# One float32 matmul per weight product in place of a high/low split of three, with a ring of twelve tiles

## The chip, the cores and the metric

The kernel runs on one core of a Trainium2 chip. The metric is the device time in microseconds of one execution; the profile is of one execution of the same program.

## What is computed

Two blocks of a network on a sequence of 256 positions with 1024 channels, everything in float32. The first block, cut from its reference:

```
h = rms_norm(x, attn_norm_w)
z, xbc, dt_raw, q, k, v, g_ssd, g_att = split_columns(h @ w_in)            # 1024 x 7440
y_ssd = ssd_mixer(z, xbc, dt_raw, ...) @ w_ssd_out                          # 1024 x 1024
y_att = moba_attention(rope(q), rope(k), v) @ w_attn_out                    # 1024 x 1024
x = x + (sigmoid(g_ssd) * y_ssd + sigmoid(g_att) * y_att) @ w_out           # 1024 x 1024
h = rms_norm(x, moe_norm_w)
for g in range(4):                                                          # 4 groups of 8 experts
    hid = silu(einsum("bld,edf->blef", h, w_gate[g])) * einsum("bld,edf->blef", h, w_up[g])
    out = out + einsum("blef,ble,efd->bld", hid, comb[:, :, g], w_down[g])  # 256 wide
gate = sigmoid(rms_norm(x, ple_norm_w) @ w_ple_gate)                        # 1024 x 1024
```

The second block has an in-projection of 1024 x 7168, a causal convolution of 31 taps, a token shift with interpolation of three of its outputs, a recurrent mixer of 16 heads, three products of 1024 x 1024, and a feed-forward 1024 x 4096 x 1024 with a squared relu. Every weight is read once, some 228 MB in all, and the moving rows of a product are always the 256 positions.

## The kernel before

**Tiles of weights.** Weights are read in the order of use as tiles of 128 partitions x 1024 float32 (512 KB; 496 KB in the first in-projection), numbered by n from Q_IN to Q_END (lines 40 to 55). A tile holds two of the eight 128-row slices of a matrix by 512 columns (`pair_view`), in the experts half gate and half up (`gu_loads`), or one slice by 1024 columns. SyncE issues the loads (`load`) into a ring of 4 tiles, `raw`, which in the experts has two more tiles (`MOE_RING`, in `proj`). A load waits until the tile that it overwrites has been split, and one expert tile is two transfers.

**The split.** ScalarE copies each tile into `whi` (type float32r; `split_high`, line 270), then GpSimd, or for every second tile of the experts VectorE, writes raw minus whi into `wlo` (`split_low`, line 275). The other operand of a product, `t0` or `t1`, is split alike: TensorE transposes the activations into PSUM (class `Turn`, line 353), ScalarE writes the high half (line 364) and VectorE the low one (lines 372, 374). A product is then three matmuls that add up in PSUM (`times`):

```
nc.tensor.matmul(dst, hi, wh, start=first, stop=False)             # L281
nc.tensor.matmul(dst, hi, wl, start=False, stop=False)             # L282
return nc.tensor.matmul(dst, lo, wh, start=False, stop=last)       # L283
```

`wide_quarter` does this for one tile: two slices by two halves of the positions, so four products of 512 columns. The down part of the experts (lines 1397 to 1399) and the second part of the feed-forward (lines 2739 to 2741) do it in place. All other matmuls, transposes among them, have plain float32 operands.

**Order of the work.** Each engine has one program, written out stage by stage, and semaphores between them. `quarter_done` counts the tiles that TensorE has used. In the first in-projection (15 column tiles of four weight tiles; `pe_in`) TensorE puts parts of the mixer between the column tiles: after the fourth the transposes of xbc, after the seventh the decay sums (line 651), which wait for VectorE's convolution of four taps (lines 737, 739), and the transposes back (line 664). Then come the output product of the mixer, attention (a chain of small operations, lines 1050 to 1078), two products of 8 tiles, the router (`act_router`, `pe_router`, `dve_router`), and the experts. In the experts a block does the gate and up of expert E + 1 (4 tiles) and the down part of expert E (2 tiles); after the sixth expert of a group the rows of the next group are gathered (line 1341), and after the first of the next one the sum is scattered back (line 1446). Experts and feed-forward are loops (`Fori`) on all engines.

In the second in-projection (14 column tiles, `pe_in2`) VectorE first mixes the shifted rows (line 1990), then runs the convolution's 31 taps over seven slices (lines 2002, 2005; 217 operations, 120 of them first). From the ninth column tile on, ScalarE copies each result (line 1905) and starts a transfer from `proj` to `work` that moves it down by one row (line 1910); VectorE waits for it, subtracts (line 1956), multiplies with a row that ScalarE had loaded (line 1957) and adds (line 1960), and does 20 or 15 more operations of the convolution before the next one. ScalarE loads the row of the next column tile but one only when line 1957 has used the buffer, and this stands in its program before the next copy and transfer. The heads (`step_loop`, lines 2207 to 2283) and the feed-forward (`pe_out2`) end the kernel. GpSimd, besides splitting, rotates part of q and k (`pool_rotations`) and does a part of the heads (`pool_heads`).

Of the kernel before, what the change touches and what calls it, by code (L numbers as in the profile page):

```python
# [9 lines left out]
F32R = mybir.dt.float32r  # L10
# [18 lines left out]
RING = 4  # L29
MOE_RING = 6  # L30
# [118 lines left out]
JOB = 6 * 8  # L149


def split_by_vector(n):

    return Q_MOE - MOE_RING <= n < Q_PLE and n % 2 == 1


def slot(n):

    return (n - Q_MOE) % MOE_RING if Q_MOE <= n < Q_PLE else n % RING

RAW_DONE, LOW_DONE = [], []
_shown = [0] * MOE_RING
for _n in range(Q_END):
    _shown[slot(_n)] += 32 if Q_MOE <= _n < Q_PLE else 16
    RAW_DONE.append(_shown[slot(_n)])
    LOW_DONE.append(sum(split_by_vector(m) == split_by_vector(_n) for m in range(_n + 1)))


def at_turn(counts, n, i, per):

    if not per:
        return counts[n]
    span = JOB if per < JOB and JOB % per == 0 and n + JOB < Q_PLE and n >= Q_MOE - MOE_RING else per
    return counts[n] + (counts[n + span] - counts[n]) * per // span * i
# [6 lines left out]
def build(nc, A, out):  # L184
    ctx = ExitStack()
    with ctx:
# [8 lines left out]
        whi = sb("whi", [P, RING, QF], F32R)  # L195
        wlo = sb("wlo", [P, RING, QF], F32R)
# [4 lines left out]
        t0h = sb("t0h", [P, KC, SEQ], F32R)  # L201
        t0l = sb("t0l", [P, KC, SEQ], F32R)
        t1h = sb("t1h", [P, 4, SEQ], F32R)
        t1l = sb("t1l", [P, 4, SEQ], F32R)
# [30 lines left out]
        raw_full = [sem(f"raw_full{s}") for s in range(MOE_RING)]  # L235
        hi_ready = sem("hi_ready")
        lo_by_pool = sem("lo_by_pool")
        lo_by_dve = sem("lo_by_dve")
# [8 lines left out]

        more_raw = proj[:, :, :].rearrange("p t n -> p (t n)")[:, 12232:12232 + (MOE_RING - RING) * QF]

        def raw_of(n):  # L250

            s = slot(n)
            return raw[:, s, :] if s < RING else more_raw[:, (s - RING) * QF:(s - RING + 1) * QF]

        def wait_low(eng, n, i=0, per=0):

            eng.wait_ge(lo_by_dve if split_by_vector(n) else lo_by_pool, at_turn(LOW_DONE, n, i, per))
# [8 lines left out]
        def split_high(act, n, i=0, per=0, width=QF):  # L266
            s = n % RING
            act.wait_ge(raw_full[slot(n)], at_turn(RAW_DONE, n, i, per))
            wait_from(act, quarter_done, n - RING + 1 + per * i)
            nc.scalar.activation(whi[:, s, 0:width], raw_of(n)[:, 0:width], ACT.Copy).then_inc(hi_ready, 1)  # L270

        def split_low(eng, n, i=0, per=0, width=QF):
            s = n % RING
            eng.wait_ge(hi_ready, n + 1 + per * i)
            ins = (nc.vector if split_by_vector(n) else nc.gpsimd).tensor_tensor(  # L275
                wlo[:, s, 0:width], raw_of(n)[:, 0:width], whi[:, s, 0:width].bitcast(F32), ALU.subtract)
            ins.then_inc(lo_by_dve if split_by_vector(n) else lo_by_pool, 1)

        def times(dst, hi, lo, wh, wl, first, last):

            nc.tensor.matmul(dst, hi, wh, start=first, stop=False)  # L281
            nc.tensor.matmul(dst, hi, wl, start=False, stop=False)  # L282
            return nc.tensor.matmul(dst, lo, wh, start=False, stop=last)  # L283

        def pair_view(buf, n, width):
            return buf[:, n % RING, 0:2 * width].rearrange("p (k n) -> p k n", k=2)

        def wide_quarter(pe, n, q, dst, hi, lo, width=TW, i=0, per=0, begun=False):


            wait_low(pe, n, i, per)
            wh, wl = pair_view(whi, n, width), pair_view(wlo, n, width)
            for t in range(NT):
                for kk in range(2):
                    k = 2 * q + kk
                    mm = times(dst[t][:, 0:width], hi[:, k, t * P:(t + 1) * P], lo[:, k, t * P:(t + 1) * P],
                               wh[:, kk, :], wl[:, kk, :], k == 0 and not begun, k == KC - 1)
            mm.then_inc(quarter_done, 1)

        def load_square(sp, n, w, quarters=range(8), order="(p k) n -> p k n"):  # L300

            v = w.rearrange(order, k=KC)
            for j in quarters:
                c, q, m = j // 4, j % 4, n + j
                load(sp, m, [(pair_view(raw, m, TW), v[:, 2 * q:2 * q + 2, c * TW:(c + 1) * TW])])

        def square_product(pe, n, hi, lo, waits, turn=None):
# [4 lines left out]
            for c in range(2):  # L312
                for q in range(4):
                    if turn is not None and c == 0:
                        pe.wait_ge(*turn.done(2 * q + 2))
# [2639 lines left out]
```

## Time and profile before

| | before |
|---|---|
| time, median of 3 runs | 1740.38 us (1737.1 to 1743.37) |
| span of the profiled execution | 1741.1 us; no other time is given for that execution |
| instructions | 21017 |
| busy: ScalarE | 724.3 us, 42% |
| busy: VectorE | 932.0 us, 54% |
| moved by DMA | 239.91 MB, 138 GB/s over the span |
| GpSimd's line 275 | 331 subtractions of 128x1024 or 128x992, 856 us |
| the chain that ended last, by engine | TensorE 47%, VectorE 16%, GpSimd 15%, issue 13%, DMA 6%, ScalarE 3% |

The busy share says how long an engine had work in progress, matmuls overlapping each other counted once. The distance between the starts of two matmuls of one kind is what one costs in a row; the mean duration is longer, because they are pipelined. The granted clock is that of TensorE, as a share of its full speed. The DMA share is the mean busy share of 16 engines.

### The profile page before, as it was taken

The page shows a single profiled execution, that of the slowest core. Times are in us where ns is not written, and L with a number is a line of the kernel's source. Part 1 is how long each engine was busy: PE and PEld are TensorE (multiplying, and loading weights), DVE is VectorE, ACT ScalarE, POOL GpSimd, SP SyncE. Part 2 cuts the span into 40 slices and gives each one's busy share as a digit, 9 for nine tenths or more (in the row PEclk, how much of TensorE's full clock was granted, in tenths as well). Part 3 has the DMA queues.
Part 4 walks back from the last instruction along what each step waited for, and adds up shares of the span by engine and source line. Part 5 has one row for each costly group of instructions (what it writes and reads, how often), then busy time and mean ns, then how long its engine had stood idle before and what let it go on. Part 6 is the DMA issues. An engine that isn't in the chain of part 4 may idle for free.

```text
span 1741.1 us, 21017 instructions
## 1 busy us (share of the span) xinstructions
PE 1448.3 (83%) x6952; PEld 1180.4 (68%) x6952; DVE 932.0 (54%) x1343; ACT 724.3 (42%) x1212; POOL 896.3 (51%) x423
## 2 busy tenths in 40 slices
PE   6989987958988888797599983364899999879997
PEld 5878876747656667565477762253799997768885
DVE  1553444356978788794506995338566665320102
ACT  4455554334645455464543312224222332433433
POOL 6867574414867667683576532240300001748784
PEclk9989986989999999999899986685999999989998
DMA  6545440344977777683364332231200001535652
GB/s 218 176 132 157 127 142 0 97 143 142 301 227 259 232 244 255 226 291 117 121 209 146 116 102 74 74 108 36 85 2 0 0 0 59 161 100 177 192 180 85
DMA packets 126193, 239.91 MB, mean 138 GB/s; under 512 B 15236, under 2 KB 31286, under 8 KB 125996
## 3 DMA queue, kind: packets, MB, share of 16 engines
q1 hardware_dynamic: 116672, 228.17, 40.8%
q10 hardware_dynamic: 9453, 10.84, 2.0%
q8 instruction: 41, 0.67, 0.2%
q14 instruction: 27, 0.22, 0.0%
HBM read 234.79 MB, written 1.05 MB: 135 GB/s over the span
## 4 chain that ended last, share of the span: by engine, by line
PE 47%; DVE 16%; POOL 15%; issue 13%; DMA 6%; ACT 3%; ACTq 0%; POOLq 0%; DVEq 0%
POOL wlo L275 15%; PE bank L281 8%; PE bank L282 8%; PE bank L283 8%; DMA work<-proj 6%; DVE work L2005 5%; PE bank L2223 3%; PE bank L2241 2%; PE bank L2237 2%; PE bank L2207 2%; PE bank L2739 2%; PE bank L2741 2%; PE bank L2740 2%; DVE work L739 2%; DVE proj L1990 2%
## 5 line engine op out<-in xcount | busy, mean ns | idle before, releaser
L275 POOL TENSOR_TENSOR wlo<-raw,whi 128x1024 fp32r<-128x1024 f32 (+1 forms) x299 | 750.2, 2523 | 576.5 <-ACT whi L270 576.0
L281 PE MATMUL bank<-whi,t0h 128*128 128x512 f32 (+1 forms) x1072 | 447.1, 417 | 94.8 <-POOL wlo L275 71.2
L270 ACT ACTIVATE whi<-raw 128x1024 fp32r<-128x1024 f32 (+1 forms) x366 | 376.6, 1053 | 312.1 <-PE bank L283 230.2
L282 PE MATMUL bank<-wlo,t0h 128*128 128x512 f32 (+1 forms) x1072 | 432.6, 404 | 0.0
L283 PE MATMUL bank<-whi,t0l 128*128 128x512 f32 (+1 forms) x1072 | 431.9, 403 | 0.0
L281 PEld LDWEIGHTS bank<-whi,t0h 128*128 128x128 f32 x1072 | 209.3, 195 | 164.0 <-issue 80.1
L283 PEld LDWEIGHTS bank<-whi,t0l 128*128 128x128 f32 x1072 | 208.6, 195 | 49.5
L282 PEld LDWEIGHTS bank<-wlo,t0h 128*128 128x128 f32 x1072 | 208.7, 195 | 45.3 <-issue 1.7
L275 DVE TENSOR_TENSOR wlo<-raw,whi 128x1024 fp32r<-128x1024 f32 x67 | 185.3, 2767 | 39.4 <-ACT whi L270 39.2
L275 POOL TENSOR_TENSOR wlo<-proj,whi 128x1024 fp32r<-128x1024 f32 x32 | 105.8, 3308 | 30.9 <-ACT whi L270 30.9
L2005 DVE SCALAR_TENSOR_TENSOR work<-work,proj 128x256 f32<-128x256 f32 x210 | 113.1, 597 | 2.0
L2482 POOL TENSOR_TENSOR proj<-proj,small x8 | 5.1, 638 | 205.2 <-PE bank L2283 205.2
L275 DVE TENSOR_TENSOR wlo<-proj,whi 128x1024 fp32r<-128x1024 f32 x32 | 94.5, 2953 | 2.4 <-ACT whi L270 2.1
L1397 PE MATMUL bank<-whi,t1h 128*128 128x512 f32 x128 | 54.1, 423 | 32.7 <-POOL wlo L275 32.7
L2564 DVE TENSOR_TENSOR work<-bank,const 128x256 f32<-128x256 f32 x112 | 46.7, 423 | 63.8 <-PE bank L2223 60.8
L353 PE MATMUL bank<-const,work 128*128 128x128 f32 x128 | 27.3, 400 | 55.7 <-DVE work L433 45.5
L270 ACT ACTIVATE whi<-proj 128x1024 fp32r<-128x1024 f32 x64 | 67.4, 1055 | 10.0 <-PE bank L283 7.2
L2854 DVE TENSOR_TENSOR t1l<-bank,t1h 128x512 fp32r<-128x512 f32 x16 | 10.3, 686 | 112.9 <-ACT t1h L2811 112.9
L353 PEld LDWEIGHTS bank<-const,work 128*128 128x128 f32 x128 | 24.9, 220 | 58.1 <-DVE work L433 33.6
L1397 PEld LDWEIGHTS bank<-whi,t1h 128*128 128x128 f32 x128 | 24.4, 190 | 50.4 <-issue 26.4
L2241 PE MATMUL bank<-work 128*128 128x64 f32 x384 | 57.6, 276 | 0.7 <-DVE work L2564 0.7
L2408 ACT COPY work<-bank 128x128 f32<-128x128 f32 x80 | 21.4, 268 | 83.3 <-PE bank L2241 83.3
(416 smaller groups left out, 2142.5 us busy)
## 6 DMA issues: line engine op xcount, KB each, us to landing
raw<-in_w_ff SPq DMA_DIRECT2D x64, 512.0 KB, 3.5
raw<-in_w_exp_down SPq DMA_DIRECT2D x124, 256.0 KB, 3.9
raw<-in_w_in SPq DMA_DIRECT2D x60, 496.0 KB, 3.5
raw<-in_w_in SPq DMA_DIRECT2D x56, 512.0 KB, 3.4
raw<-in_w_exp_gate SPq DMA_DIRECT2D x66, 256.0 KB, 4.1
raw<-in_w_exp_up SPq DMA_DIRECT2D x66, 256.0 KB, 5.1
proj<-in_w_exp_gate SPq DMA_DIRECT2D x62, 256.0 KB, 3.5
proj<-in_w_exp_up SPq DMA_DIRECT2D x62, 256.0 KB, 5.1
```

Source lines behind the costliest of these rows:

```text
L270: nc.scalar.activation(whi[:, s, 0:width], raw_of(n)[:, 0:width], ACT.Copy).then_inc(hi_ready, 1)
L275: ins = (nc.vector if split_by_vector(n) else nc.gpsimd).tensor_tensor(wlo[:, s, 0:width], raw_of(n)[:, 0:width], whi[:, s, 0:width].bitca ...
L281: nc.tensor.matmul(dst, hi, wh, start=first, stop=False)
L282: nc.tensor.matmul(dst, hi, wl, start=False, stop=False)
L283: return nc.tensor.matmul(dst, lo, wh, start=False, stop=last)
L353: tr = nc.tensor.transpose(bank[4 + b][:, at:at + P], self.src[:, t, :, 2 * b + kk], ident)
L739: ins = nc.vector.scalar_tensor_tensor(out=convT[:, c, :], in0=xbcT[:, c, w:w + SEQ], scalar=tap, in1=convT[:, c, :], op0=ALU.mult, op1=AL ...
L1397: nc.tensor.matmul(bank[4 + h][:, :], hh, whi[:, s, f], start=first, stop=False, skip_group_check=True)
L2005: ins = nc.vector.scalar_tensor_tensor(out=cvT[:, c, :], in0=uT[:, c, w:w + SEQ], scalar=tap, in1=cvT[:, c, :], op0=ALU.mult, op1=ALU.add)
L2223: mm = nc.tensor.matmul(bank[g][:, v * P:(v + 1) * P], gram[b][:, u, 0:P], ident if lev == 0 else Xm[:, u, :], start=True, stop=True)
L2241: mm = nc.tensor.matmul(bank[2 + g][:, P + v * 64:P + (v + 1) * 64], Ym[:, u, :], odd[:, u], start=True, stop=True)
L2564: nc.vector.tensor_tensor((Xm if lev == 0 else Ym)[:, 2 * g:2 * g + 2, :], bank[g][:, 0:2 * P].rearrange("p (u s) -> p u s", u=2), con(f"l ...
```

## The change

All weight products are made of one float32 matmul, with the loaded tile as its moving operand and an unsplit `t0` or `t1` as the stationary one. The buffers whi, wlo, t0l and t1l, both kinds of splitting and their semaphores go. The ring has 12 tiles for the whole kernel, and a load waits only for the tile's last use by TensorE. An expert's gate and up weights are tiles of their own (four slices by 256 columns, one transfer, contiguous 4 KB per partition), so that a matmul there has 256 columns instead of 512. The transposed activations are copied out of PSUM by ScalarE (banks 0 and 2) and VectorE (banks 1 and 3) at once. The loops over experts and over the feed-forward are written out on every engine. Three rows that were loaded into ring slots before the heads get buffers of their own (`held`). The router's weights are used as loaded, and its loads wait for the transposes before them. The diff, cut to its core:

```diff
-RING = 4
-MOE_RING = 6
+RING = 12
...
-        def load(sp, n, pairs, i=0, per=0):
-            before = n - (MOE_RING if Q_MOE + RING <= n < Q_PLE else RING)
-            if before >= 0:
-                wait_low(sp, before, i, per)
-            for dst, src in pairs:
-                sp.dma_start(dst, src).then_inc(raw_full[slot(n)], 16)
+        def load(sp, n, dst, src):
+            wait_from(sp, quarter_done, n - RING + 1)
+            sp.dma_start(dst, src).then_inc(raw_full[slot(n)], 16)
...
+            wait_raw(pe, n)
+            w = pair_view(n, width)
             for t in range(NT):
                 for kk in range(2):
                     k = 2 * q + kk
-                    mm = times(dst[t][:, 0:width], hi[:, k, t * P:(t + 1) * P], lo[:, k, t * P:(t + 1) * P],
-                               wh[:, kk, :], wl[:, kk, :], k == 0 and not begun, k == KC - 1)
+                    mm = nc.tensor.matmul(dst[t][:, 0:width], x[:, k, t * P:(t + 1) * P], w[:, kk, :],
+                                          start=k == 0 and not begun, stop=k == KC - 1)
             mm.then_inc(quarter_done, 1)
...
+            def act(self, act, used, banks=(0, 2)):
+                    if self.gain is None:
+                        ins = nc.scalar.copy(self.x[:, 2 * b:2 * b + 2, :].rearrange("p k s -> p (k s)"), bank[4 + b][:, :])
...
+            def dve(self, dve, used, banks=(1, 3)):
+                        ins = nc.vector.tensor_tensor(self.x[:, r, :], src,
+                                                      self.gain[:, r].unsqueeze(2).to_broadcast([P, 2, SEQ]), ALU.mult)
...
+        def gate_up_load(sp, n, e, q):
+
+            v = A[("w_exp_gate", "w_exp_up")[q // 2]][0].rearrange("g e (p k) n -> p (g e) k n", k=KC)
+            load(sp, n, raw[:, slot(n), :].rearrange("p (a k n) -> p a k n", a=1, k=4),
+                 v[:, e:e + 1, 4 * (q % 2):4 * (q % 2) + 4, :])
...
+                w = raw[:, slot(n), :].rearrange("p (k n) -> p k n", k=4)
+                dst = bank[E % 2][:, DE * (q // 2):DE * (q // 2) + DE]
+                par = (E // EG) % 2
+                for kk in range(4):
+                    k = 4 * (q % 2) + kk
+                    mm = nc.tensor.matmul(dst, t0[:, k, par * P:(par + 1) * P], w[:, kk, :], start=k == 0,
+                                          stop=k == KC - 1)
...
-            pool_stream(pool)
+            pool_rotations(pool)
+            pool_heads(pool)
```

## Rows read from the trace of the kernel before

**Rows 1.** The page, part 1: busy us (share of the span) and instructions of an engine.

```profile
PE 1448.3 (83%) x6952; PEld 1180.4 (68%) x6952; DVE 932.0 (54%) x1343; ACT 724.3 (42%) x1212; POOL 896.3 (51%) x423
```

**Rows 2.** Windows cut at the stages; columns as in its first line.

```profile
core 0: us, PE busy (x) PEld busy (x) DVE busy (x) ACT busy (x) POOL busy (x), PEclk, DMA share, GB/s
0.00:218.60 218.60, 194.40 (x926) 163.38 (x926) 87.55 (x160) 110.11 (x152) 146.39 (x67) 0.97 0.53 163
218.60:309.20 90.60, 75.27 (x352) 62.76 (x352) 39.74 (x116) 44.31 (x110) 54.32 (x82) 0.71 0.21 65
309.20:363.30 54.10, 50.97 (x224) 41.36 (x224) 17.37 (x29) 17.68 (x28) 21.80 (x9) 0.96 0.47 145
363.30:404.20 40.90, 20.18 (x116) 19.47 (x115) 26.26 (x81) 14.71 (x29) 5.65 (x2) 0.75 0.18 64
404.20:806.20 402.00, 344.14 (x1368) 260.04 (x1368) 318.00 (x188) 216.28 (x259) 285.16 (x96) 0.98 0.74 243
806.20:871.60 65.40, 39.89 (x164) 30.75 (x164) 31.75 (x46) 34.78 (x62) 31.11 (x13) 0.84 0.37 117
871.60:1192.90 321.30, 219.01 (x865) 168.47 (x865) 186.97 (x278) 90.42 (x132) 139.51 (x56) 0.83 0.36 114
1192.90:1245.80 52.90, 39.84 (x156) 31.52 (x156) 33.07 (x44) 24.47 (x41) 16.99 (x8) 0.76 0.23 80
1245.80:1467.00 221.20, 218.11 (x1717) 203.54 (x1717) 133.68 (x318) 64.86 (x250) 13.91 (x17) 0.99 0.00 1
1467.00:1536.00 69.00, 53.67 (x234) 43.28 (x232) 31.40 (x44) 26.99 (x47) 39.27 (x16) 0.90 0.51 160
1536.00:1731.20 195.20, 192.77 (x836) 155.85 (x836) 20.77 (x32) 76.92 (x93) 142.22 (x60) 0.98 0.47 151
```

**Rows 3.** Groups of TensorE by form: count, busy us, mean ns, idle before.

```profile
L281 PE MATMUL bank<-whi,t0h 128*128 128x512 f32 x832 | 351.7, 423 | 92.8 <-POOL wlo L275 71.2 <-DVE wlo L275 6.2 <-DVE t0l L1363 6.2
...
L281 PE MATMUL bank<-whi,t0h 128*128 128x496 f32 x240 | 95.4, 398 | 2.0 <-DVE t0l L374 2.0
```

**Rows 4.** TensorE's timeline (start us, us) and the scatter's line with min/median/max ns.

```profile
517.08 0.40 PE L1398 MATMUL bank<-wlo,t1h 128*128 128x512 f32 x1
517.32 0.40 PE L1399 MATMUL bank<-whi,t1l 128*128 128x512 f32 x1
517.55 2.74 PE L1446 MATMUL bank<-proj 128*128 128x512 f32 x6
...
L1446 PE MATMUL bank<-proj x32: 591/592/1002, 517.5 to 810.7; 128*128 128x512 f32 x32
...
1148.47 10.53 PE L1872 MATMUL bank<-work 128*128 128x256 f32 x48
```

**Rows 5.** VectorE's timeline in the two convolutions.

```profile
70.32 29.05 DVE L739 SCALAR_TENSOR_TENSOR work<-work,small 128x256 f32<-128x256 f32 x30
...
969.98 74.68 DVE L2005 SCALAR_TENSOR_TENSOR work<-work,proj 128x256 f32<-128x256 f32 x116
...
1114.60 6.38 DVE L2005 SCALAR_TENSOR_TENSOR work<-work,proj 128x256 f32<-128x256 f32 x15
```

**Rows 6.** Windows at the start and in the experts; columns as in rows 2.

```profile
4.00:6.00 2.00, 0.00 (x0) 0.00 (x0) 0.00 (x0) 0.00 (x0) 0.00 (x0) 1.00 1.01 420
...
8.00:10.00 2.00, 0.00 (x0) 0.00 (x0) 0.00 (x0) 1.17 (x3) 0.00 (x0) 1.00 1.03 393
430.00:480.00 50.00, 44.79 (x183) 34.31 (x183) 45.87 (x24) 30.29 (x37) 43.51 (x15) 1.00 0.91 302
```

**Rows 7.** VectorE's timeline in the router and before the second in-projection.

```profile
377.74 5.83 DVE L275 TENSOR_TENSOR wlo<-raw,whi 128x1024 fp32r<-128x1024 f32 x2 [0.83 <-ACT whi L270]
...
861.03 5.10 DVE L433 TENSOR_SCALAR work<-xres,small 128x1024 f32<-128x1024 f32 x2
```

**Rows 8.** The chain that ended last, one round of the shift: start us, us, what.

```profile
1081.27 26.09 DMA work<-proj
...
1107.55 1.89 DVE work L1956
1109.46 3.31 DVE work L1957
...
1113.18 1.08 ACT proj L1905 x2
...
1115.10 24.07 DMA work<-proj
```

More of the change, by code:

```diff
@@ L143, in wait_from @@
         eng.wait_ge(sem, value)
-JOB = 6 * 8
-def split_by_vector(n):
-    return Q_MOE - MOE_RING <= n < Q_PLE and n % 2 == 1
 def slot(n):
-    return (n - Q_MOE) % MOE_RING if Q_MOE <= n < Q_PLE else n % RING
-RAW_DONE, LOW_DONE = [], []
-_shown = [0] * MOE_RING
+    return n % RING
+RAW_DONE = []
+_shown = [0] * RING
 for _n in range(Q_END):
-    _shown[slot(_n)] += 32 if Q_MOE <= _n < Q_PLE else 16
+    _shown[slot(_n)] += 16
     RAW_DONE.append(_shown[slot(_n)])
[L169 to L177, printed above, removed]
 NORMS = ["attn_norm_w", "moe_norm_w", "ple_norm_w", "ssd_norm_w", "norm_mix_g_2", "norm_ff_g_2",
@@ L266, in split_high @@
[L266 to L292, printed above, removed]
+        def wait_raw(eng, n):
+            eng.wait_ge(raw_full[slot(n)], RAW_DONE[n])
@@ L373, in dve @@
                     else:
-                        ins = nc.vector.scalar_tensor_tensor(out=self.lo[:, k, :], in0=self.part(k),
-                                                             scalar=self.gain[:, k:k + 1], in1=hi,
-                                                             op0=ALU.mult, op1=ALU.subtract)
-                    ins.then_inc(self.low, 1)
+                        nc.scalar.activation(self.x[:, 2 * b, :], self.part(2 * b), ACT.Identity,
+                                             scale=self.gain[:, 2 * b:2 * b + 1])
@@ L1400, in down @@
                                           skip_group_check=True)
                 mm.then_inc(quarter_done, 1)
-            def block(J, E, b, m, i=0, per=0, first=False, last=False):
+            pe.wait_ge(xg_ready, 2)
+            for q in range(4):
+                gate_up(Q_MOE + q, q, 0)
+            for E in range(N_EXP):
+                J, e = E // EG, E % EG
+                m = first_of(E)
+                if e == EG - 1 and E < N_EXP - 1:
+                    pe.wait_ge(xg_ready, 2 * (J + 2))
@@ L2756, in pe_out2, with first_at, second_at @@
                 for c in range(4):
-                    second(Q_FF + 8 + c, c, j, j, 8)
-            turn(FF_J - 1)
-            for c in range(4):
-                second(Q_END - 4 + c, c, FF_J - 1, last=c == 3)
+                    second(j, c)
+        def first_at(j):
+            return Q_FF + (8 * j - 4 if j else 0)
+        def second_at(j):
+            return Q_FF + 8 * j + (8 if j < FF_J - 1 else 4)
         def sp_ff(sp):
```

648 lines of the change are left out of this document (207 added, 441 removed).

## The prediction

> **What bounds the kernel now.** I read the page's busy times first, then windows cut at the stages, then the matmul groups, and last single stretches of the timeline, the waits' chain and the DMA windows. TensorE is busy most of the span and GpSimd half of it [rows 1]; cut by stage [rows 2], TensorE is near full wherever weights stream (0 to 218.6, 309.2 to 363.3, 404.2 to 806.2, 1536.0 to 1731.2) and in the heads stage (1245.8 to 1467.0), which uses no streamed weights. It is far from full in the router (363.3 to 404.2) and the second in-projection (871.6 to 1192.9). So a cheaper product pays in some stages by its full size and in others only as far as the stage's other chain allows.
>
> **One product.** Two of the split's matmuls start 0.235 us apart (517.08, 517.32, then 517.55), so a product of three is 0.70 us. The scatter's matmuls in the same stretch, plain float32 and of the same 128x512 size, each with its own weight load, run six in 2.74 us; less one duration of 0.59 that is (2.74 - 0.59)/5 = 0.43 us each. A 256-column one costs 10.53/48 = 0.22 us [rows 4]. A tile of four products thus falls from 2.80 to 1.72 us; one of 496 columns, by columns, from 2.71 to 1.67. There are 832 products of 512 columns and 240 of 496 [rows 3], and by the code 128 each in the experts' down part (32 x 2 tiles) and the feed-forward's second part (8 x 4 tiles of four); of the 832, 256 are gate and up, which become 512 of 256 columns (16 x 0.22 = 3.5 us per expert against 5.6).
> The Trainium skill ("FP8 and Floating Point Precision", TensorE Precision Notes) speaks against this: it gives true float32 four passes of the array. By it, four times the split's 0.235, a product would be near 0.9 us and the change a loss. By that rule, the trace disagrees: its float32 matmul takes less than two of the split's [rows 4].
> The sum goes by the row, 0.43.
>
> **What GpSimd's subtractions cost VectorE.** In the first conv thirty scalar_tensor_tensor of 128x256 take 29.05 us while GpSimd subtracts, nearly 1 us each; in the second conv 116 take 74.68 us (0.64 each) in the stretch where GpSimd works, and 15 take 6.38 (0.43) where it is quiet [rows 5]. I take 0.41 to 0.43 once GpSimd's splits are gone, because the same line shows it; the dear bound is that nothing changes (0.64 and 0.97).
>
> **The transfers.** With the ring of 4 to 6 tiles the experts' stretch 430 to 480 moves 302 GB/s at a share of 0.91, or 331 at a full share. In the first microseconds, when eight transfers or so are queued, the same engines move 420 and, when the large constants are in, still 393 GB/s with the in-projection's rows of under 2 KB [rows 6]. Twelve tiles outstanding resemble the latter: I take 395, with 331 and 420 as ends.
> The Trainium skill ("DMA: Bandwidth & Descriptors", Measured) gives 341 GB/s for a single 1 MB transfer, and more only for 16 MB. By it the experts' 94.4 MB would take 277 us instead of 239.
>
> **Stage by stage** (before [rows 2], then after; all in us of the span).
> - *0 to 218.6, in-projection and first mixer.* The product starts at about 17 (18.7 before: the pass that makes t0's low half is gone). Four column tiles at 16 x 0.417 = 6.7 end at 44, transposes 2.5, three more end at 66.5. VectorE's conv, begun at 44 and with 3.5 of copies, takes 15 instead of 32 and is done at 63, so the wait in front of the decay sums nearly goes; silu and the transposes back end at 73 (109.5 before). Then 8 tiles, 53.4, and the 18 us of small matmuls between them end at about 144. The group norm behind the last state step loses some 5 us of VectorE wait: the next transposes start at 148, against 218.6. Gain 70. The transfers need 305 GB/s here, below what I take: not the bound.
> - *218.6 to 309.2.* Eight tiles, 8.6, of which half a us returns while the clock is low. The attention behind them (245.6 to 309.2) is a chain of small operations that had no split in it. Gain 8.
> - *309.2 to 363.3.* Sixteen tiles, 17.3, and a little in two turns. Gain 18.
> - *Router, 40.9.* Two VectorE splits, 5.8, stand ahead of its chain [rows 7], the router weights' split and a norm part queued behind ScalarE's splits some 3, 16 fewer logit matmuls and the low half of the turn 2. Its six loads are now issued later and into a queue with 12 tiles; they have some 20 us before the logits. Gain 11.
> - *Experts, 402.* TensorE needs 3.5 + 4 x 0.43 + 0.2 = 5.4 per expert, 173; four gathers of 7.1 and scatters of 5 to 6 make about 222. The transfers need 192 tiles less the 12 that the long router lets in: 94.4 MB, at 395 GB/s 239, plus filling: 243. The ring absorbs the gathers. So the bound passes from GpSimd, VectorE and TensorE together to the DMA, narrowly. At 331 GB/s it is 285 + 4, at 420 it is TensorE and DMA together, 230. Gain 159.
> - *806.2 to 871.6.* Ten tiles, 11; three ScalarE splits on the chain of the norm, 3; the norm's scaling, two operations in 5.10 us [rows 7] that take about 1.5 alone, and the turn's low half, together 6; another half each from two waits. Gain 21.
> - *Second in-projection, 321.3.* TensorE's fifth tile ends at +36 instead of +61. VectorE then does the token shift's mixing and 120 conv steps: 10 + 50 at the free rate, where it took 27 + 76. It is done at +103, where it was +173. The ninth tile, whose shift starts the chain, is done at about +87, its shift transfer has landed at about +112. Now a serial chain rules that no part of the change shortens: a transfer of 24 to 26 us from proj to work, two VectorE operations, the ring row's load and two copies, then the next transfer [rows 8]. A round was 31.3; with VectorE's operations at 1.2 instead of 3.3 it is 28.5. Four rounds end at +226.5, then 3.7 and 36 conv steps, 15.5: +246. Bounds: with VectorE still slow +290; with the 70 us before the chain kept, +315; nothing suggests less than +235. Gain 75.
> - *Conv output and first head, 52.9.* Eight tiles save 9, a contended VectorE pair 2 to 3. Gain 12.
> - *Heads, 221.2.* Small float32 matmuls, untouched. 0.
> - *1467.0 to 1536.0.* Sixteen tiles 17, contended merge, norm and turn 6, splits in the turn 1. Gain 24.
> - *Feed-forward, 195.2.* 64 x 1.72 = 110, eight turns of 0.9, two waits at the end of a few us: 122. TensorE stays the bound (2.1 MB per 6.9 us are 304 GB/s). The four clearing matmuls go. Gain 73.
> - *End, 9.9.* 0.
> Gains: 70 + 8 + 18 + 11 + 159 + 21 + 75 + 12 + 24 + 73 = 471. The profiled span of 1741.1 stands 0.7 above the median of the runs; the span after is 1270, and so is, within a us, the time I forecast.
> Edits costed at nothing: the unrolled loops (as many matmuls or fewer per us than the in-projection, which is unrolled already, issues without a gap); the ACT engine's 366 + 64 splits, except where named, since ScalarE waits on them more than it works; the three rows moved to their own tile, which saves SP a wait long before their use.
>
> **Rivals.**
> 1. *The transfers do not speed up.* Each tile is still 512 KB, and 331 GB/s may be what full engines give on long streams; for it stands the long stretch of [rows 6], against it the start. Experts 289 instead of 243, and slack of 4 us elsewhere: 1320. Chance 0.14.
> The Trainium skill's 341 GB/s, cited above, lies near this rival's rate.
> 2. *VectorE's slow operations are not GpSimd's doing.* Then the conv waits stay: +17 in the first stage, +44 in the second in-projection, some 14 in norms, merges and turns: 1345. Against it: [rows 5] show one line at two speeds. Chance 0.05.
> 3. *TensorE falls to its lower clock in the experts, because it now idles between tiles.* The stage shows a granted share of 0.98 at 86% busy, the router's stretch 0.75 at half busy [rows 2]. A tile would take 1.75 us against 1.33 from the DMA: at half of the time low, about +35: 1305. Chance 0.08, inside the range.
> 4. *Slower: float32 costs four passes when its moving operand is a streamed tile.* Products at twice the row's 0.43, or 0.86, add 0.16 to each 0.70: +41 in the feed-forward, +37 in the first stage (which keeps the conv's gain of 25 at most), +31 in the eight-tile squares, and the experts need 390, about as now; against this stand some 30 us of freed VectorE and splits. About 1800. It decides from 0.70 us per product on, a little above with the other gains. The row at 0.43 excludes it unless the operand matters. Chance 0.02.
> 5. *The change gives more:* both clocks full, 420 GB/s, and more slack out of the turns than I count: below 1235. Chance 0.06.
>
> **How the numbers follow.** My forecast of 1270 has 0.65 for its own range, 1235 to 1305. The range reaches to rival 1 and some of rival 2: 1235 to 1335. Every case but the fourth is far beyond the 0.3% (5 us) that a measurement of this kernel can tell: faster 0.975, same 0.005, slower 0.02.
>
> **What would show it.** Right: the weight matmuls start 0.43 us apart; GpSimd under 150 us busy; the first conv's thirty operations in 12 to 13 us; 380 to 400 GB/s at a share near 1 in the experts, with TensorE waiting for the DMA; rounds of 28 to 29 us in the shift chain; the feed-forward at about 122. Wrong: starts 0.8 apart; DMA at 300 with its share full; VectorE's operations still near 0.6; code loads that leave TensorE waiting for nothing the profile names.

## The result and the profile after

The changed kernel takes 1802.24 us (median of 4 runs, 1800.67 to 1804.88) against 1741.88 us before (4 runs beside them): a ratio of 1.035, 95% interval 1.0321 to 1.0378. It is slower, where 1270 us and a chance of 0.02 for slower had been forecast. The span of the profiled execution is 1802.7 us. The miss is 532 us, so a large term must be wrong.

The page, part 1, of the changed kernel, to be read beside [rows 1]:

```profile
PE 1617.0 (90%) x6116; PEld 1011.8 (56%) x6116; DVE 495.3 (27%) x1123; ACT 275.4 (15%) x724; POOL 42.7 (2%) x92
```

The engines that had split are relieved: GpSimd fell from 896 to 43 us (under 150 was forecast), VectorE from 932 to 495, ScalarE from 724 to 275. TensorE was to fall with them and rose from 1448 to 1617. Its instructions went from 6952 to 6116 only. By the counts of [rows 3] and the steps of the prediction, 1328 products of three matmuls became 1584 products, so some 2,400 instructions should have gone, not 836. Windows cut at the same stages, to be read beside [rows 2] and with its columns:

```profile
0.00:243.30 243.30, 228.54 (x686) 115.66 (x687) 59.74 (x154) 44.31 (x82) 0.20 (x4) 1.00 0.54 159
243.30:336.30 93.00, 76.45 (x322) 53.32 (x320) 35.93 (x110) 35.34 (x100) 30.78 (x72) 0.76 0.17 52
336.30:401.40 65.10, 62.27 (x160) 30.90 (x160) 9.39 (x14) 5.17 (x10) 0.00 (x0) 0.95 0.43 136
401.40:434.10 32.70, 21.03 (x107) 17.79 (x107) 16.59 (x70) 6.56 (x14) 0.00 (x0) 0.74 0.05 16
434.10:813.70 379.60, 379.10 (x1496) 285.88 (x1496) 33.30 (x59) 24.21 (x64) 0.00 (x0) 1.00 0.78 263
813.70:874.90 61.20, 44.75 (x124) 22.25 (x124) 19.06 (x33) 20.07 (x42) 0.00 (x0) 0.90 0.35 103
874.90:1218.30 343.40, 251.00 (x640) 122.03 (x640) 128.93 (x276) 34.67 (x76) 0.00 (x0) 0.86 0.37 112
1218.30:1266.10 47.80, 40.31 (x124) 22.43 (x124) 24.92 (x40) 14.02 (x29) 0.00 (x0) 0.87 0.29 89
1266.10:1488.80 222.70, 219.57 (x1717) 204.49 (x1718) 133.66 (x318) 64.45 (x248) 11.68 (x16) 0.99 0.01 3
1488.80:1561.40 72.60, 63.95 (x169) 31.47 (x168) 17.99 (x27) 6.41 (x17) 0.00 (x0) 0.92 0.41 123
1561.40:1792.80 231.40, 230.03 (x576) 105.60 (x576) 10.34 (x16) 17.38 (x33) 0.00 (x0) 0.99 0.38 118
```

Set TensorE's busy time beside the length of the stage: in the experts TensorE is busy for 379.1 of 379.6 us, in the feed-forward for 230 of 231, in the first stage for 229 of 243. The DMA share in the experts is 0.78, where a share near 1 and a TensorE that waits had been forecast: here TensorE doesn't wait for weights. Whatever is wrong is in TensorE. Its groups by form, of the changed kernel:

```profile
L240 PE MATMUL bank<-raw,t 128*128 128x512 f32 x1152 | 513.0, 604 | 43.4 <-ACT proj L1687 38.2 <-DVE t L326 2.2 <-ACT work L2553 1.2
L1247 PE MATMUL bank<-raw,t 128*128 128x256 f32 x1024 | 231.3, 379 | 0.6 <-issue 0.6
L240 PE MATMUL bank<-raw,t 128*128 128x496 f32 x480 | 204.1, 585 | 1.0 <-DVE t L326 1.0
L1263 PE MATMUL bank<-raw,t 128*128 128x512 f32 x256 | 115.2, 592 | 0.5 <-ACT t L1320 0.5
L2496 PE MATMUL bank<-raw,t 128*128 128x512 f32 x256 | 111.3, 593 | 0.2 <-ACT t L2558 0.2
```

And its timeline in the experts (start us, us), and one of its transposes:

```profile
472.81 3.62 PE L1247 MATMUL bank<-raw,t 128*128 128x256 f32 x16
...
479.94 3.60 PE L1263 MATMUL bank<-raw,t 128*128 128x512 f32 x8
...
L1254 PE MATMUL bank<-const,proj 128*128 128x128 f32 x64 | 12.5, 277 | 0.0
```

The counts hold the answer. The code has 240 products of 496 columns; the trace has 480 instructions. It has 512 gate and up products and 1024 instructions, 128 down products and 256, 128 in the feed-forward's second part and 256. **One float32 matmul of the source is two instructions on TensorE**, each with a weight load of its own (PEld counts 6116 too). A transpose is one: line 1254 is run 64 times and stands at x64. Two for each of 1584 products are 3168 instructions in place of 3984, 816 fewer, close to the 836 of the page. The durations were right: eight of line 1263 last 3.60 us, so (3.60 - 0.59)/7 = 0.43 us each, as forecast, and sixteen of line 1247 last 3.62, so (3.62 - 0.38)/15 = 0.22. But a product is two of them, 0.86 us, against 0.70 for the three of the split. The row from which 0.43 came says it too, once one counts: line 1446 stands in [rows 4] with x32, and the code issues 16 matmuls there.

### The profile page after: what moved, and what is told of

Its sections match the earlier page's. It is cut to its first block, busy times and chain, and to the rows that moved or that the text cites. A ratio compares the mean times of both kernels' runs of the same rounds, so it can differ in the third digit from the quotient of the medians.

```text
span 1802.7 us, 15975 instructions
## 1 busy us (share of the span) xinstructions
PE 1617.0 (90%) x6116; PEld 1011.8 (56%) x6116; DVE 495.3 (27%) x1123; ACT 275.4 (15%) x724; POOL 42.7 (2%) x92
## 4 chain that ended last, share of the span: by engine, by line
PE 82%; DMA 7%; DVE 5%; issue 3%; ACT 2%; ACTq 0%; DVEq 0%
PE bank L240 35%; PE bank L1247 12%; DMA work<-proj 7%; PE bank L2496 6%; PE bank L1263 6%; PE bank L1989 3%; PE bank L2007 2%; PE bank L1220 2%; PE bank L2003 2%; PE bank L298 2%; PE bank L1973 2%; DVE work L1783 1%; PE bank L1304 1%; PE bank L1631 1%; ACT work L358 1%
## 5 line engine op out<-in xcount | busy, mean ns | idle before, releaser
L240 PE MATMUL bank<-raw,t 128*128 128x512 f32 (+1 forms) x1632 | 717.0, 598 | 44.5 <-ACT proj L1687 38.2
L240 PEld LDWEIGHTS bank<-raw,t 128*128 128x128 f32 x1632 | 312.7, 194 | 427.3 <-issue 381.2
L1247 PE MATMUL bank<-raw,t 128*128 128x256 f32 x1024 | 231.3, 379 | 0.6 <-issue 0.6
L1247 PEld LDWEIGHTS bank<-raw,t 128*128 128x128 f32 x1024 | 192.1, 190 | 36.4 <-issue 13.1
L1263 PE MATMUL bank<-raw,t 128*128 128x512 f32 x256 | 115.2, 592 | 0.5 <-ACT t L1320 0.5
L2496 PE MATMUL bank<-raw,t 128*128 128x512 f32 x256 | 111.3, 593 | 0.2 <-ACT t L2558 0.2
L1328 DVE SCALAR_TENSOR_TENSOR proj<-bank,proj 128x256 f32<-128x256 f32 x32 | 15.5, 483 | 282.6 <-ACT proj L1318 282.6
L1783 DVE SCALAR_TENSOR_TENSOR work<-work,proj 128x256 f32<-128x256 f32 x210 | 87.9, 477 | 2.0
L2496 PEld LDWEIGHTS bank<-raw,t 128*128 128x128 f32 x256 | 48.6, 190 | 61.1 <-issue 60.7
L1263 PEld LDWEIGHTS bank<-raw,t 128*128 128x128 f32 x256 | 48.6, 190 | 48.2 <-issue 45.9
L2007 PE MATMUL bank<-work 128*128 128x64 f32 x384 | 57.6, 276 | 0.7 <-DVE work L2324 0.7
L1989 PE MATMUL bank<-work 128*128 128x128 f32 x384 | 55.6, 287 | 0.1
L2007 PEld LDWEIGHTS bank<-work 128*128 128x128 f32 x384 | 49.9, 192 | 3.2 <-issue 2.3
L1989 PEld LDWEIGHTS bank<-work 128*128 128x128 f32 x384 | 48.1, 191 | 3.6 <-issue 2.3
L1320 ACT COPY t<-bank 128x256 f32<-128x256 f32 x32 | 11.9, 372 | 248.8 <-PE bank L1254 248.8
L2003 PE MATMUL bank<-work 128*128 128x64 f32 x320 | 48.6, 274 | 0.1
L298 PEld LDWEIGHTS bank<-const,work 128*128 128x128 f32 x128 | 23.5, 216 | 43.7 <-DVE work L384 22.2
L2003 PEld LDWEIGHTS bank<-work 128*128 128x128 f32 x320 | 42.2, 192 | 1.3 <-DVE work L2324 0.7
```

What stands on the lines that cost most here:

```text
L240: mm = nc.tensor.matmul(dst[t][:, 0:width], x[:, k, t * P:(t + 1) * P], w[:, kk, :], start=k == 0 and not begun, stop=k == KC - 1)
L298: tr = nc.tensor.transpose(bank[4 + b][:, at:at + P], self.src[:, t, :, 2 * b + kk], ident)
L1247: mm = nc.tensor.matmul(dst, t0[:, k, par * P:(par + 1) * P], w[:, kk, :], start=k == 0, stop=k == KC - 1)
L1263: mm = nc.tensor.matmul(bank[4 + h][:, :], t1[:, 2 * (E % 2) + c, 0:P], raw[:, slot(n), 512 * h:512 * h + 512], start=E % EG == 0 and c == ...
L1783: ins = nc.vector.scalar_tensor_tensor(out=cvT[:, c, :], in0=uT[:, c, w:w + SEQ], scalar=tap, in1=cvT[:, c, :], op0=ALU.mult, op1=ALU.add)
L1989: mm = nc.tensor.matmul(bank[g][:, v * P:(v + 1) * P], gram[b][:, u, 0:P], ident if lev == 0 else Xm[:, u, :], start=True, stop=True)
```

## The experiments

**Is it the price, and is it the operand's type?** The first theory, A: a float32 product of 512 columns costs 0.86 us wherever it stands. The rival, B: some other part of the change (no splits, the ring, the unrolled code) brings the time. Three variants of the changed kernel vary the price with all else kept, and e3 puts it into the kernel before. In e1 and e2 a product is two bfloat16 matmuls, or one, on the upper 16 bits of both operands (the lower bits are left out; in e1 the second has a tile of zeros as its stationary operand), and e9, below, has three:

```
+        def product(dst, x, w, start, stop, **kw):
+            x, w = (a.bitcast(BF16).rearrange("p (n h) -> p n h", h=2)[:, :, 1] for a in (x, w))
+            for i in range(2):
+                mm = nc.tensor.matmul(dst, zero[:, :] if i else x, w, start=start and i == 0,
+                                      stop=stop and i == 1, **kw)
...
-                    mm = nc.tensor.matmul(dst[t][:, 0:width], x[:, k, t * P:(t + 1) * P], w[:, kk, :],
+                    mm = product(dst[t][:, 0:width], x[:, k, t * P:(t + 1) * P], w[:, kk, :],
```

> The changed kernel with each weight product made of two bfloat16 matmuls instead of the one float32 matmul: the first on the upper 16 bits of both operands, the second with a stationary tile of zeros (so the low bits are left out of the result). Two such matmuls of 512 columns cost about 2 x 0.216 = 0.43 us, the price that the prediction took for the float32 one. Theory A (the source's one float32 matmul is two TensorE instructions of 0.43 each, and that is the whole error): everything else of the prediction holds and the time is 1260 to 1310, experts 240 to 250, feed-forward 120 to 125. Theory B (something else than the product's price, such as the ring, the unrolled code or the new copies, made the changed kernel slow): it stays above 1600.

> The same with one bfloat16 matmul on the upper 16 bits per product, 0.22 us: TensorE no longer bounds any streaming stage. It shows what bounds next. Theory A: the experts stay at the transfers' 235 to 250 us at 395 GB/s (289 if full engines give 331), the feed-forward falls to the transfers' 85 to 95, the in-projection to 105 plus the mixer's chain; in all 1130 to 1180. Theory B: above 1500.

Measured: e1 1327.11 us (1326.39 to 1328.43), ratio to before 0.7623 (0.7609 to 0.7636); e2 1166.61 us (one run). e1 is 17 us above the 1260 to 1310 expected, e2 inside its 1130 to 1180. Two of e1's matmuls of 512 columns cost 0.45 us, near the 0.43 that the prediction had used, and at that price the change gives 414 of the 471 us that the prediction said. That makes e1 the kernel by which its other terms can be read, stage by stage, in the section after this one.

e3 goes the other way: the kernel before with all its splits, and one float32 matmul of the two high halves where it had three (the low halves' products are left out):

```
-            nc.tensor.matmul(dst, hi, wh, start=first, stop=False)
-            nc.tensor.matmul(dst, hi, wl, start=False, stop=False)
-            return nc.tensor.matmul(dst, lo, wh, start=False, stop=last)
+            return nc.tensor.matmul(dst, hi.bitcast(F32), wh.bitcast(F32), start=first, stop=last)
```

> The kernel before with all its splits, rings and waits kept, but each product made of one float32 matmul of the high halves (the low halves are still written and are left out of the result). Theory A: a product goes from 0.70 to 0.86: +37 in the first in-projection, +41 in the feed-forward, +31 in the six squares, some +25 in the second in-projection, +30 to +60 in the experts, 5 elsewhere: 1890 to 1940. Theory B (float32 at 0.43 as the prediction had it): 1450 to 1600.

Measured: 1872.25 us (1870.34 to 1874.22), ratio 1.0749 (1.0729 to 1.0769), slower as theory A has it and 18 us below its 1890 to 1940. Fewer matmuls in the source, a slower kernel. The groups of e3, against [rows 3]:

```profile
L281 PE MATMUL bank<-whi,t0h 128*128 128x512 f32 x1664 | 755.5, 608 | 65.0 <-POOL wlo L275 46.6 <-DVE wlo L275 4.9 <-DVE t0l L1361 4.1
L281 PE MATMUL bank<-whi,t0h 128*128 128x496 f32 x480 | 203.6, 584 | 2.0 <-DVE t0l L372 2.0
```

832 and 240 in [rows 3] have become 1664 and 480 for the same calls. So the doubling comes with the type of the operands and not with the streamed tile.

> The changed kernel with three bfloat16 matmuls per product (the upper halves once and a tile of zeros twice; the low bits are left out), so about 0.65 us a product, near the 0.70 of the kernel before: what the rest of the change (no splits, ring of 12, unrolled loops) is worth at the old price. e2, e1 and the changed kernel (one, two and, by count of instructions, four passes) took 1167, 1327 and 1802, so if the price of a product alone sets the difference, three give 1550 to 1585, about 170 below the kernel before, and the product at 0.86 then costs 220 to 250 on top. If the changed kernel had another fault than the price, three passes would stay above 1650.

Measured: 1575.41 us (1573.97 to 1576.85), ratio 0.9044 (0.9029 to 0.9059), inside the range given. The four kernels with the change, whose product of 512 columns costs 0.23, 0.45, 0.68 and 0.86 us (e2, e1, e9 and the changed kernel), take 1167, 1327, 1575 and 1802: 160, 248 and 227 us a step. The first step is smaller because the experts of both e2 and e1 wait for the DMA: from VectorE's product of gate and up for the first expert to that for the last they take 234 and 236 us, against 298 in e9 and 365 in the changed kernel. With e3 there is a table of two by two:

| | product near 0.7 | product 0.86 |
|---|---|---|
| splits kept | 1741 (before) | 1872 (e3) |
| splits gone, ring of 12, unrolled | 1575 (e9; its product is 0.68) | 1802 (after) |

The rest of the change is worth 166 us at the old price (of which at most some 0.02 x 1328 products = 27 belong to 0.68 against 0.70), and 70 at the new one, where TensorE covers nearly everything. The dearer product takes back 131 to 227. B falls. What the unrolled loops are worth by themselves no run shows.

**The ring.** e4 is the changed kernel with `RING = 4` in place of 12, e5 is e1 with the same line.

> The changed kernel with a ring of 4 tiles instead of 12. Theory A: TensorE bounds the streams at 3.44 us per 512 KB tile (152 GB/s) and 1.73 per expert tile (303 GB/s), so the ring matters only in the experts, where three tiles in flight at about 4 to 5 us each just reach that: +0 to +25 there. A side question: the shift chain's transfers took 30, 35, 34, 29 and 24 us against 24 to 26 before. If the tiles that the long ring lets through at that time slow the one transfer, they come back to 24 to 26 and the stage gains 20 to 30, giving 1780 to 1800 in all; if not, they stay at 29 to 35 and the time is 1800 to 1830.

> The kernel of e1 (two bfloat16 matmuls in place of each product, the low bits left out) with a ring of 4 tiles instead of 12. If the depth of the ring is what lets the transfers run at 409 GB/s in the experts, the experts fall back towards 300 to 331 GB/s and take 290 to 315 us instead of 246; the token shift's transfers, which seem to share an engine with the weight tiles, lose some 10 us; the kernel takes 1360 to 1400 against e1's 1327. If the depth doesn't matter and only the freed tiles' earlier release did, 1320 to 1335.

Measured: e4 1816.86 us (1815.51 to 1821.31), ratio 1.0439 (1.0417 to 1.0462), 15 us above the changed kernel. e5 1449.70 us (1447.14 to 1450.89), ratio 0.8323 (0.831 to 0.8335), 123 us above e1, where 33 to 73 had been expected. A window of 50 us in the experts of the changed kernel:

```profile
450.00:500.00 50.00, 50.00 (x202) 37.43 (x201) 1.93 (x4) 3.40 (x9) 0.00 (x0) 1.00 0.86 294
```

A window of 50 us in e1's experts:

```profile
430.00:480.00 50.00, 47.44 (x294) 32.73 (x292) 7.04 (x12) 4.54 (x12) 0.00 (x0) 1.00 1.03 409
```

And in e5, with its whole stage of the experts under it:

```profile
430.00:480.00 50.00, 38.78 (x204) 26.18 (x204) 3.80 (x7) 3.33 (x9) 0.00 (x0) 0.87 0.76 249
...
303.20:680.20 377.00, 278.52 (x1524) 175.01 (x1524) 37.71 (x67) 28.38 (x72) 0.00 (x0) 0.91 0.79 268
```

With 12 tiles and a cheap product the engines are full at 409 GB/s; with 4 neither they (0.76) nor TensorE (39 of 50 us) are: each waits for the other, and TensorE's granted clock is 0.87 where it was 1.00. A tile lands 5.7 to 6.8 us after its issue there (medians by matrix); at 249 GB/s that is, as an estimate, three of the four tiles under way and the fourth in use. The depth of the ring was worth 131 us in the experts (377 against 246.2) where the product is cheap, and 15 where it is dear (394.9 against 379.6, by windows of e4 and after). What a change gives depends on the others made with it.

**The shift's transfer.** e1 stands 37 us above the forecast in the second in-projection, and the chain of waits shows why. The last four transfers from proj to work in e1 (start us, us), against [rows 8]:

```profile
723.74 33.87 DMA work<-proj
...
762.63 33.42 DMA work<-proj
...
801.07 29.75 DMA work<-proj
...
835.83 23.50 DMA work<-proj
```

They took 23.5, 26.1, 24.1 and 24.4 us before. In the changed kernel they take 35.1, 33.5, 29.3 and 23.6. Windows over these four:

```profile
1062.10:1097.20 35.10, 24.16 (x57) 10.41 (x55) 5.86 (x15) 3.91 (x10) 0.00 (x0) 0.91 0.44 136
1102.20:1135.80 33.60, 14.72 (x32) 6.13 (x30) 5.75 (x14) 2.44 (x8) 0.00 (x0) 0.75 0.39 127
1140.80:1170.10 29.30, 26.24 (x80) 15.60 (x78) 5.71 (x14) 2.44 (x8) 0.00 (x0) 0.91 0.28 91
1175.10:1198.70 23.60, 4.71 (x14) 3.61 (x14) 5.78 (x14) 3.10 (x9) 0.00 (x0) 0.62 0.07 25
```

Over two of before:

```profile
1081.30:1107.40 26.10, 8.50 (x31) 6.46 (x30) 7.62 (x17) 6.23 (x12) 6.08 (x3) 0.69 0.21 66
1115.10:1139.20 24.10, 6.00 (x19) 4.47 (x18) 5.74 (x14) 6.23 (x12) 6.21 (x3) 0.65 0.16 51
```

The last of the four is alone, and moves 25 GB/s at a DMA share of 0.07: one engine in sixteen. During the others weight tiles pass beside it: rate by time, less the 0.5 MB of the transfer, is 4.3, 3.8 and 2.2 MB, or 8, 7 and 4 tiles, for 11.6, 10.1 and 5.8 us more than 23.5, some 1.4 us for each tile; a sixteenth of a tile, 32 KB, takes 1.3 us at 25 GB/s. Before, 1.2 and 0.7 MB passed, two tiles and one, for 2.6 and 0.6 us more, so less for each. The depth of the ring has little part in it: in e4 the four take 34.8, 29.4, 29.2 and 23.5 us, 117 in sum against 122. The Trainium skill ("DMA: Bandwidth & Descriptors", on why a DMA increments its semaphore by 16) says that a transfer uses the largest number of engines up to 16 that divides the slowest dimension of both sides, and that 127 partitions put everything on one. The trace agrees: 0.07. If that is the cause, 112 rows and 15 rows will go otherwise. The edit, in the changed kernel (e6), the kernel before (e7) and e1 (e8):

```
-                    act.dma_start(s[1:P, :, :], rkv[0:P - 1, :, f]).then_inc(shift_loaded[p % 2], 16)
+                    act.dma_start(s[1:113, :, :], rkv[0:112, :, f]).then_inc(shift_loaded[p % 2], 16)
+                    act.dma_start(s[113:P, :, :], rkv[112:P - 1, :, f]).then_inc(shift_loaded[p % 2], 16)
...
-            dve.wait_ge(shift_loaded[p % 2], 32 * ((p - RKV2) // 2 + 1))
+            dve.wait_ge(shift_loaded[p % 2], 48 * ((p - RKV2) // 2 + 1))
```

> The changed kernel, with the token shift's transfer of 127 rows issued as one of 112 and one of 15. Theory: the 127 rows go through one of the 16 DMA engines (508 KB at 22 to 25 GB/s in the trace), and every weight tile that is under way adds its share of that engine. Cut so that the rows spread over engines, the transfer takes 2 to 6 us instead of 23.5 to 35; the rounds fall to TensorE's 14 us, the second in-projection from 343 to 250-265, the kernel to 1710-1730. If the transfers are slow for another reason (both ends in SBUF), nothing changes: 1795 to 1805.

> The kernel before with the same cut of the shift's transfer. There the four transfers take 23.5 to 26 us in rounds of 31; with short ones VectorE sets the round (3.7 for the shift and 6.4 for its part of the conv, slower beside GpSimd), so the second in-projection ends 70 to 90 us earlier: 1650 to 1675. If the one engine is not the reason, 1735 to 1745.

> The kernel of e1 (two bfloat16 matmuls per product, the low bits left out) with the same cut. In e1 the rounds are 28 to 39 us, of which 24 to 34 the transfer; here VectorE's 10 us or TensorE's 7 set them, so 283 us of the second in-projection become 165 to 185: the kernel at 1205 to 1235. If the engine is not the reason, 1320 to 1330.

Measured: e6 1707.61 us (1705.45 to 1708.99), ratio 0.9812 (0.9797 to 0.9827), 95 us below the changed kernel and 2 us below the range expected. e7 1691.04 us (1688.8 to 1691.93), ratio 0.971 (0.9697 to 0.9724). e8 1225.63 us (1220.53 to 1226.36), ratio 0.7032 (0.7017 to 0.7047), 101 below e1 and inside its range. e6 and e7 leave nothing of the computation out and take less than both kernels of this case, e7 2.9% and e6 1.9% less than the kernel before. The second in-projection of e6 as a window:

```profile
876.00:1120.40 244.40, 239.13 (x640) 115.56 (x640) 128.87 (x276) 34.79 (x76) 0.00 (x0) 0.99 0.54 158
```

The issues of the transfer's larger part between 1070 and 1120 us (KB each, median us to landing):

```profile
work<-proj ACTq DMA_DIRECT2D x3, 448.0 KB, 4.6
```

448 KB in 4.6 us are 100 GB/s, four times what the one engine moved. The only one that is in the chain of waits there, while weight tiles keep the engines full (a share of 1.03), takes longer:

```profile
1090.91 9.98 DMA work<-proj
```

The second in-projection went from 343.4 to 244.4 us, and TensorE is busy for 239 of them: the chain of transfers is gone and TensorE is the bound. In e8 it takes 179.6 us where e1 took 283.1. e7 gave 50 us where 70 to 90 were expected. VectorE's timeline of e7 says what took its place:

```profile
1058.38 3.26 DVE L1958 TENSOR_TENSOR work<-work 128x1024 f32<-128x1024 f32 x1
1061.67 3.28 DVE L1961 TENSOR_TENSOR proj<-proj,work 128x1024 f32<-128x1024 f32 x1
...
1065.53 18.62 DVE L2006 SCALAR_TENSOR_TENSOR work<-work,proj 128x256 f32<-128x256 f32 x15
...
1107.57 14.61 DVE L2006 SCALAR_TENSOR_TENSOR work<-work,proj 128x256 f32<-128x256 f32 x15
```

The fifteen operations take 18.62 and 14.61 us, in [rows 5] the like take 6.38. Windows of e7 over these two:

```profile
1065.50:1084.10 18.60, 18.60 (x82) 14.96 (x81) 18.46 (x16) 6.59 (x12) 14.43 (x6) 1.00 0.74 215
...
1107.60:1122.20 14.60, 14.60 (x68) 12.60 (x67) 14.44 (x16) 6.89 (x13) 9.85 (x4) 1.00 0.67 191
```

And of before over the fifteen of [rows 5]:

```profile
1114.60:1121.00 6.40, 2.80 (x12) 1.91 (x11) 6.24 (x16) 0.00 (x0) 0.00 (x0) 1.00 0.16 53
```

The fifth column, GpSimd, is 14.43 and 9.85 us where it was 0. Before, each round had a pause between GpSimd's splits of one column tile and the next (20 to 21 us without work), and these operations fell into it.

**GpSimd beside VectorE.** That this slows VectorE was a step of the prediction, and after shows it only by absence. e10 puts it back alone: the changed kernel with a GpSimd subtraction of 128x1024 on scratch memory behind each tile of both in-projections (for room, the ring has 9 tiles):

```
+            pool.wait_ge(quarter_done, n)
+            pool.wait_ge(burned, count)
+            nc.gpsimd.tensor_tensor(burn[:, 2, :], burn[:, 0, :], burn[:, 1, :], ALU.subtract).then_inc(burned, 1)
```

> The changed kernel with a GpSimd subtraction of 128x1024 on scratch memory behind each tile of both in-projections (116 of them; to make room the ring has 9 tiles). If GpSimd's subtractions slow VectorE through the memory they share, the first conv's 30 operations go from 12.2 us back to 20 to 30, the second conv's from 0.43 to 0.55 or more each, and the kernel takes 1805 to 1840 (in the first in-projection TensorE is full and hides it; in the second it delays the start of the shift chain). If the splits' other traffic was the cause, the operations stay at 0.41 to 0.43 and the time at 1798 to 1806.

Measured: 1816.07 us (1813.97 to 1818.56), ratio 1.0424 (1.0407 to 1.0442), 14 above the changed kernel and inside the range given; the total also has the ring of 9 in it, whose share wasn't taken apart. In the second conv 116 operations take 78.56 us, 0.68 each (0.55 or more expected); in the first, thirty take more than the 20 to 30 us expected:

```profile
80.37 35.34 DVE L666 SCALAR_TENSOR_TENSOR work<-work,small 128x256 f32<-128x256 f32 x30
```

The first conv's line in the changed kernel (min/median/max ns of one):

```profile
L658 DVE SCALAR_TENSOR_TENSOR work<-work,small x30: 476/480/486, 80.2 to 91.9; 128x256 f32<-128x256 f32 x30
```

Both convs' lines in e10:

```profile
L666 DVE SCALAR_TENSOR_TENSOR work<-work,small x30: 472/473/2631, 80.4 to 113.1; 128x256 f32<-128x256 f32 x30
...
L1791 DVE SCALAR_TENSOR_TENSOR work<-work,proj x210: 349/480/2606, 991.5 to 1231.7; 128x256 f32<-128x256 f32 x105
```

And the first conv's line in the kernel before:

```profile
L739 DVE SCALAR_TENSOR_TENSOR work<-work,small x30: 472/478/2628, 70.3 to 98.9; 128x256 f32<-128x256 f32 x30
```

Thirty operations took 12.2 us in the changed kernel and take 35.3 in e10. The median did not move; the longest is 2.6 us, nearly one operation and one of GpSimd's subtractions (mean 2.38 us). So VectorE isn't slowed throughout, single operations are held up for about as long as a GpSimd instruction lasts. The Trainium skill ("SBUF — State Buffer", Who interferes with whom) calls the pair of ports that the two share a lock held for a full instruction, not a shared bandwidth; the maximum of 2.6 us beside a median of 0.47 agrees. The kernel before has the same median and maximum (478 and 2628 ns), so the mean of nearly 1 us in [rows 5] was such a mixture.

## Why the prediction was wrong, point by point

**"One product" failed.** The step took 0.43 us from the starts of line 1446 and called it a product. It is the price of one instruction; a float32 product is two of them. The row at 0.43 stands; what was left out is to set the row's count beside the calls in the code. That one factor decides the sign: at 0.45 the change is 24% faster (e1), at 0.86 it is 3.5% slower. The prediction named the rule that would have caught it, the four passes of true float32 (the Trainium skill, "FP8 and Floating Point Precision", TensorE Precision Notes), and said that the trace disagreed. It doesn't: two instructions at 0.43 are 0.86, and four times the 0.23 of one of e1's bfloat16 matmuls of 512 columns are 0.91. An instruction that "takes less than two of the split's" had been compared with the wrong thing.

**Rival 4 happened**, with the wrong condition. It asked for an operand that makes float32 dear; no such operand is needed. Its sums hold: about 1800 in all (1802), the feed-forward +41 (+36 measured), the first stage at least +12 (+25), the experts 390 (379.6). That the total agrees to 2 us is partly luck: the second in-projection, 22 us longer than before, isn't in its sum, and the experts came out 10 us below it. It got 0.02 because the row was taken to exclude it.

**The other steps can be judged in e1**, where a product costs nearly what the prediction said. Its 1327 us lie outside the range of 1235 to 1305 too; its span is 54 us above the forecast, and 37 of the 54 are in one stage. Stages in us, from windows cut as above:

| stage, by its start before | before | forecast | e1 | after |
|---|---|---|---|---|
| 0, in-projection and mixer | 218.6 | 148.6 | 148.6 | 243.3 |
| 218.6, output product, attention | 90.6 | 82.6 | 81.7 | 93.0 |
| 309.2, sixteen tiles | 54.1 | 36.1 | 44.1 | 65.1 |
| 363.3, router | 40.9 | 29.9 | 27.9 | 32.7 |
| 404.2, experts | 402.0 | 243 | 246.2 | 379.6 |
| 806.2, gate and norm | 65.4 | 44.4 | 47.3 | 61.2 |
| 871.6, second in-projection | 321.3 | 246.3 | 283.1 | 343.4 |
| 1192.9, conv output | 52.9 | 40.9 | 38.2 | 47.8 |
| 1245.8, heads | 221.2 | 221.2 | 224.0 | 222.7 |
| 1467.0, sixteen tiles | 69.0 | 45 | 46.1 | 72.6 |
| 1536.0, feed-forward | 195.2 | 122.2 | 127.2 | 231.4 |
| end | 9.9 | 9.9 | 9.9 | 9.9 |

Four of e1's rows, among them the two largest differences:

```profile
0.00:148.60 148.60, 131.09 (x687) 69.98 (x687) 59.78 (x154) 45.24 (x84) 0.41 (x5) 1.00 0.81 260
...
230.30:274.40 44.10, 36.85 (x160) 19.07 (x160) 12.59 (x21) 6.70 (x15) 0.00 (x0) 0.89 0.64 212
...
302.30:548.50 246.20, 234.51 (x1496) 162.88 (x1496) 33.30 (x59) 24.21 (x64) 0.00 (x0) 0.99 1.01 400
...
595.80:878.90 283.10, 163.52 (x640) 80.96 (x640) 128.94 (x276) 34.67 (x76) 0.00 (x0) 0.77 0.43 136
```

- *Experts:* right, and by the mechanism: the DMA full (share 1.01), 400 GB/s over the stage against 395 taken, TensorE waiting for it. Rival 1, at 331 GB/s, falls. The Trainium skill ("DMA: Bandwidth & Descriptors", Measured) gives 341 GB/s for a single 1 MB transfer; tiles of half that size passed it here, at 400 GB/s with a ring of twelve.
- *First stage, router, gate and norm:* right to within 3 us. VectorE's thirty operations take 12.2 us in after, 12 to 13 forecast, and 116 of the second conv 49.5, or 0.43 each. Rival 2 falls, by e10.
- *Second in-projection:* 37 us too little. The step "a transfer of 24 to 26 us" took the duration of before for a constant. It is that of a transfer with one engine nearly to itself; with the weights coming in closer behind one another it takes up to 34. The four rounds were 28 to 39 us and took 141 in sum, forecast 114 (four of 28.5): 27 of the 37. The other 10 or so stand before them: the ninth tile was copied at 92 us into the stage (87 forecast), and its own transfer took some 29. VectorE's operations were at 1.24, as forecast.
- *309.2:* 8 us too little: its tiles take 1.88 us of TensorE (30.0 us for sixteen) at a granted clock of 0.89, for 1.72 forecast, and TensorE is idle for 7.3 us of the stage where it was 3.1 before.
- *Feed-forward:* 5 us too little: the bfloat16 matmuls of 512 columns there start 0.227 us apart, so a tile is 1.81 in place of 1.72, 6 us in 64 tiles.
- *Rival 3*, the lower clock in the experts, did not come: 0.99 in e1, 1.00 in after.

In the changed kernel the price hides most of this: with 3.4 us of TensorE per tile of 512 columns, nearly all idle time in front of line 240 (38.2 of 43.4 us) is that of the shift's chain. There VectorE starts on the shift 182 us into the stage where it was 174, and the four rounds take 142 us where they took 125: the change added to TensorE's time before the chain and to the transfers in it. So the stage became 22 us longer than before though VectorE's work in it fell from 187 to 129 us.

## What to carry to other kernels

Before a duration from the trace becomes the price of a call, divide the row's count by the calls in the code: float32 matmuls appear twice, float32 transposes once. Three float32r matmuls (0.70 us for 128x512) are cheaper than one float32 matmul (0.86), so a high/low split pays on TensorE; over the whole kernel it paid by 131 us with the splits' other work kept (before against e3) and by 17 against the kernel without it, once the shift's transfer was cut in both (e7 against e6). And look at the first dimension of each transfer on a critical chain: 127 rows in one transfer cost 23.5 us or more here, 112 and 15 rows some 5 to 10.

## What the runs showed of the hardware beyond what was expected

- A float32 matmul of 512 columns is two instructions, each with a weight load, each 0.43 us; one of 256 columns two of 0.22. A float32 transpose is one instruction.
- A transfer of 127 rows runs on one DMA engine, at 25 GB/s, and each 512 KB tile that passes meanwhile adds about 1.4 us to it where four to eight pass (less in the kernel before, where one or two do). The cut into 112 and 15 rows was worth 95 us in one kernel, 101 in another and 50 in a third, by what was the next bound.
- Twelve tiles of 512 KB in flight moved 409 GB/s, four moved 249 at a DMA share of 0.76, with TensorE as little full. By the 5.7 to 6.8 us from issue to landing about three of the four were under way (an estimate); rings between 4 and 12 were not run at the cheap price.
- A GpSimd subtraction of 2.4 us can hold one of VectorE's operations up for nearly its whole length (2.63 us against 0.47); the median of VectorE's operations stays at 0.47 us.
- The pause that one slow resource makes can be a shelter for another: shorter transfers in e7 brought 50 us and not 95, since GpSimd's splits then met VectorE's work.
